# Three kinds of 128-row tiles moved from three 256-column products per weight block to one of 512 and one of 256

## What is computed

```
u = rmsnorm(x) @ w_in                       # layer 1; z is a slice of 4096 columns of u
y = concat(y_l, y_m) * silu(z);  x = x + y @ w_out
u = rmsnorm(x) @ w_in                       # layer 2
z, xbc, dt = split(u);  y = ssd(xbc, dt) * silu(z);  x = x + norm(y) @ w_out
u = rmsnorm(x) @ w_in                       # layer 3; last 3 * 2048 columns: branch gates g0, g1, g2
mix = sigmoid(g0) * s5(u) + sigmoid(g1) * gla(u) + sigmoid(g2) * diff(u)
```

## Time and profile before

| | |
|---|---|
| median of 3 runs | 3216.04 us (3215.46 to 3218.31) |
| the profiled execution: its time, its span | 3217.17 us, 3215.4 us |
| granted TensorE clock, mean | 0.988 |
| busy, share of the span | TensorE 96%, its weight loads 89%, VectorE 72%, ScalarE 57%, GpSimd 17% |
| HBM, mean over the span | 173 GB/s |

### The profile page before, as it was taken

The page is one execution under the profiler, slowest core; times in us unless marked ns, Lnnn a source line. Parts: engine busy times, 40 slices in busy tenths (PEclk is TensorE's granted clock), DMA queues, the critical chain, the costliest instruction groups (busy, mean ns, idle before and its releaser), DMA issues.

```text
span 3215.4 us, 53602 instructions
## 1 busy us (share of the span) xinstructions
PE 3089.6 (96%) x21726; PEld 2853.5 (89%) x21726; DVE 2301.2 (72%) x3156; ACT 1830.6 (57%) x2363; POOL 532.8 (17%) x640
## 2 busy tenths in 40 slices
PE   7999898999999999999988999999999999999998
PEld 6889888889999999889877899999998888888886
DVE  6655788657778877675866787786656888888544
ACT  5554677645666676645556454444445666666443
POOL 2000000000000000114743565760001000000000
PEclk9999999999999999999999999999999999999999
DMA  5445434556555555556433444456555555555554
GB/s 198 141 155 179 142 133 142 198 191 217 181 174 184 178 177 201 192 177 208 156 115 112 142 153 157 170 173 210 184 184 190 190 190 190 190 190 190 190 190 138
DMA packets 158473, 560.50 MB, mean 174 GB/s; under 512 B 17600, under 2 KB 25856, under 8 KB 157712
## 3 DMA queue, kind: packets, MB, share of 16 engines
q1 hardware_dynamic: 158224, 557.06, 51.8%
HBM read 550.64 MB, written 6.36 MB: 173 GB/s over the span
## 4 chain that ended last, share of the span: by engine, by line
PE 67%; DVE 17%; ACT 10%; issue 3%; POOL 2%; DMA 0%; SPq 0%; DVEq 0%; ACTq 0%; POOLq 0%
PE ps L565 67%; DVE WL L1336 5%; ACT WH L912 3%; ACT L902 3%; DVE XV L1310 2%; DVE YB L1310 1%; ACT DB L902 1%; DVE XV L1306 1%; DVE YS L1299 1%; DVE DB L1299 1%; ACT RS L902 1%; DVE XP L1299 0%; POOL PB L1922 0%; DVE ZB L1299 0%; DVE XC L1310 0%
## 5 line engine op out<-in xcount | busy, mean ns | idle before, releaser
L565 PE MATMUL ps<-XN,WH 128*128 128x256 f32 (+1 forms) x8864 | 1855.8, 303 | 34.2 <-DVE XN L1310 17.7
L912 ACT ACTIVATE WH<-RAW 128x1024 fp32r<-128x1024 f32 x1010 | 1064.9, 1058 | 1119.7 <-PE ps L565 1078.9
L1336 DVE TENSOR_TENSOR WL<-RAW,WH 128x1024 fp32r<-128x1024 f32 x1010 | 1259.6, 1253 | 444.8 <-ACT WH L912 439.3
L565 PEld LDWEIGHTS ps<-XN,WH 128*128 128x128 f32 x8864 | 1434.2, 192 | 112.9 <-DVE XN L1310 18.6
L565 PE MATMUL ps<-XN,WL 128*128 128x256 f32 x5120 | 1444.5, 282 | 0.0
L565 PEld LDWEIGHTS ps<-XN,WL 128*128 128x128 f32 x5120 | 980.9, 192 | 0.0
L565 PE MATMUL ps<-YS,WH 128*128 128x512 f32 (+1 forms) x1088 | 372.9, 390 | 9.7 <-DVE WL L1336 5.1
L565 PE MATMUL ps<-YS,WL 128*128 128x256 f32 x1056 | 297.3, 281 | 0.0
L1922 POOL TENSOR_TENSOR RSB<-RSB,SQ 128x256 f32<-128x256 f32 x75 | 75.9, 1012 | 1224.7 <-ACT SQ L902 1223.5
L565 PEld LDWEIGHTS ps<-YS,WH 128*128 128x128 f32 x1088 | 204.5, 190 | 55.3 <-DVE WL L1336 6.7
L565 PE MATMUL ps<-HS,WH 128*128 128x512 f32 x688 | 238.6, 392 | 0.0
(11 more groups left out here) (332 smaller groups left out, 3347.2 us busy)
## 6 DMA issues: line engine op xcount, KB each, us to landing
RAW<-in_w SPq DMA_DIRECT2D x1010, 512.0 KB, 3.4
CSB<-sums SPq DMA_DIRECT2D x64, 128.0 KB, 3.8
X<-scratch SPq DMA_DIRECT2D x2, 2048.0 KB, 8.2
X<-in_x SPq DMA_DIRECT2D x4, 512.0 KB, 8.3
X<-in_x SPq DMA_DIRECT2D x1, 2048.0 KB, 8.0
scratch<-X SPq DMA_DIRECT2D x1, 2048.0 KB, 8.6
scratch<-X SPq DMA_DIRECT2D x4, 512.0 KB, 5.4
out<-X SPq DMA_DIRECT2D x4, 512.0 KB, 2.6
```

What stands on the lines that cost most here:

```text
L565: return pe.e.matmul(dst, l, r, start=start, stop=stop, skip_group_check=True)
L912: act.e.activation(WH[:, w % NH, :], RAW[:, w % NB, :], ACT.Copy).then_inc(*act.one(("wh", w)))
L1336: dve.e.tensor_tensor(WL[:, w % NB, :], RAW[:, w % NB, :], WH[:, w % NH, :].bitcast(F32), SUB).then_inc(*dve.one(("wl", w)))
```

## The change

The z, zs and g0 tiles get form "w". Their evacuation becomes four instructions on three engines, spread over more steps: at s = 0 ScalarE copies the second half out of PSUM (`second_half`, into ZLO, ZSLO or G0LO); at s = 1 VectorE adds the first half to it (`halves`, which also frees the bank) and GpSimd multiplies by RSB, in place of VectorE's `evac` at s = 0; at s = 2 ScalarE takes Silu or Sigmoid; VectorE's product with Silu(z) goes from s = 1 to s = 3. `gg`'s product on VectorE goes from its first step to s = 2, and `gl`'s steps come one later. Each copy waits until the add before it has read the one buffer.

```diff
@@ STEPS @@
-    "xm": 2, "q": 3, "k": 3, "v": 3, "o": 1, "gates": 7, "z": 2, "lruc": 3, "xl": 2, "zl": 1, "ra": 1, "ix": 1,
-    "tail": 6, "heads": 64, "eo": 1, "dt": 1, "dts": 9, "xv": 1, "zs": 1, "ssd": 21, "oo": 1, "nx": 4,
+    "xm": 2, "q": 3, "k": 3, "v": 3, "o": 1, "gates": 7, "z": 4, "lruc": 3, "xl": 2, "zl": 1, "ra": 1, "ix": 1,
+    "tail": 6, "heads": 64, "eo": 1, "dt": 1, "dts": 9, "xv": 1, "zs": 3, "ssd": 21, "oo": 1, "nx": 4,
...
-    "dv": 1, "dq": 1, "diff": 15, "g12": 1, "gb": 1, "db": 1, "g0": 1, "gg": 1, "gl": 2, "s5": 207, "wo": 1,
+    "dv": 1, "dq": 1, "diff": 15, "g12": 1, "gb": 1, "db": 1, "g0": 3, "gg": 3, "gl": 3, "s5": 207, "wo": 1,
@@ plan @@
-        p.append(whole(tile("z", (j,), "e_w_in", 6144 + 128 * j), 16))
+        p.append(whole(tile("z", (j,), "e_w_in", 6144 + 128 * j, form="w"), 16))
-            p.append(whole(tile("zs", (g, j), "o_w_in", 512 * g + 128 * j), 16))
+            p.append(whole(tile("zs", (g, j), "o_w_in", 512 * g + 128 * j, form="w"), 16))
-        p.append(whole(tile("g0", (n,), "w_in_2", 7184 + 128 * n), 16))
+        p.append(whole(tile("g0", (n,), "w_in_2", 7184 + 128 * n, form="w"), 16))
@@ scalar @@
+            def second_half(dst, *id_):
+                act.wait_ge(*at("tile", *id_))
+                fn(dst, bank(*id_)[:, 256:512], ACT.Copy, ("half",) + id_)
             def z(j, s):
-                if s == 0 and j % 4 == 3:
+                if s == 0:
+                    if j:
+                        act.wait_ge(*at("za", j - 1))
+                    second_half(ZLO, "z", j)
+                if s == 2 and j % 4 == 3:
                     act.wait_ge(*at("zq", j))
                     fn(ZQ, ZQ, ACT.Silu, ("zs", j // 4))
             def zs(g, j, s):
-                if j == 3:
+                if s == 0:
+                    if g + j:
+                        act.wait_ge(*at("zsa", *((g, j - 1) if j else (g - 1, 3))))
+                    second_half(ZSLO, "zs", g, j)
+                if s == 2 and j == 3:
                     act.wait_ge(*at("zsr", g))
                     fn(ZB, ZB, ACT.Silu, ("zsd_", g))
             def g0(n, s):
-                act.wait_ge(*at("g0r", n))
...
+                if s == 0:
+                    act.wait_ge(*(at("g0a", n - 1) if n else at("sy", 31)))
+                    second_half(G0LO, "g0", n)
+                if s == 2:
+                    act.wait_ge(*at("g0r", n))
...
@@ vector @@
+            def halves(dst, *id_, name):
+                dve.wait_ge(*at("half", *id_))
+                tt(dst, bank(*id_)[:, 0:256], dst_half(id_[0]), ADD, ("free",) + id_, name)
             def z(j, s):
-                if s == 0:
-                    evac(ZQ[:, j % 4, :], 0, "z", j, more=[("zq", j)])
-                if s == 1 and j % 4 == 3:
+                if s == 1:
+                    halves(ZQ[:, j % 4, :], "z", j, name=("za", j))
+                if s == 3 and j % 4 == 3:
...
             def zs(g, j, s):
-                evac(ZB[:, j, :], 1, "zs", g, j, more=[("zsr", g)])
+                if s == 1:
+                    halves(ZB[:, j, :], "zs", g, j, name=("zsa", g, j))
             def g0(n, s):
-                evac(SG[:, 2 * (n % 2), :], 2, "g0", n, more=[("g0r", n)])
+                if s == 1:
+                    halves(SG[:, 2 * (n % 2), :], "g0", n, name=("g0a", n))
             def gg(n, s):
+                if s != 2:
+                    return
...
             def gl(n, s):
-                if s == 0:
+                if s == 1:
...
-                if s == 1:
+                if s == 2:
@@ gpsimd @@
+            def z(j, s):
+                if s == 1:
+                    pool.wait_ge(*at("za", j))
+                    pool.wait_ge(*at("rs", 0))
+                    tt(ZQ[:, j % 4, :], ZQ[:, j % 4, :], RSB, MUL, ("zq", j))
+            def zs(g, j, s):
+                if s == 1:
+                    pool.wait_ge(*at("zsa", g, j))
+                    pool.wait_ge(*at("rs", 1))
+                    tt(ZB[:, j, :], ZB[:, j, :], RSB, MUL, ("zsr", g))
+            def g0(n, s):
+                if s == 1:
+                    pool.wait_ge(*at("g0a", n))
+                    pool.wait_ge(*at("rs", 2))
+                    tt(SG[:, 2 * (n % 2), :], SG[:, 2 * (n % 2), :], RSB, MUL, ("g0r", n))
```

More of the change, by code:

```diff
@@ L391, in build @@
         ONER = m("ONER", 256, rows=4)
+        ZLO = m("ZLO", 256)
         top_at = (end - 2304) // 32 * 32
@@ L431, in build @@
         CSB = [m(f"CSB{i}", 256) for i in range(NCSB)]
+        ZSLO = m("ZSLO", 256)
         assert m.at <= XT + 2048
@@ L485, in build @@
         MAG = P1[2]
+        G0LO = flat(CR)[:, 0:256]
         OB = v3(m("OB", 512), 2)
@@ L1238, in g0 @@
             def g0(n, s):
-                act.wait_ge(*at("g0r", n))
-                sl = SG[:, 2 * (n % 2), :]
-                fn(sl, sl, ACT.Sigmoid, ("g0s", n))
+                if s == 0:
[3 more added lines that the diff above has]
+                    act.wait_ge(*at("g0r", n))
+                    sl = SG[:, 2 * (n % 2), :]
+                    fn(sl, sl, ACT.Sigmoid, ("g0s", n))
             def gg(n, s):
+                if s:
+                    return
                 act.wait_ge(*at("tile", "gg", n))
@@ L1434, in gates, with dst_half @@
                     copy(AT, bank("gt")[:, 0:8], ("rc",), ("free", "gt"))
+            def halves(dst, *id_, name):
+                dve.wait_ge(*at("half", *id_))
+                tt(dst, bank(*id_)[:, 0:256], dst_half(id_[0]), ADD, ("free",) + id_, name)
+            def dst_half(kind):
+                return {"z": ZLO, "zs": ZSLO, "g0": G0LO}[kind]
             def z(j, s):
-                if s == 0:
-                    evac(ZQ[:, j % 4, :], 0, "z", j, more=[("zq", j)])
-                if s == 1 and j % 4 == 3:
+                if s == 1:
+                    halves(ZQ[:, j % 4, :], "z", j, name=("za", j))
+                if s == 3 and j % 4 == 3:
                     dve.wait_ge(*at("zs", j // 4))
@@ L1572, in zs @@
             def zs(g, j, s):
-                if g == 0 and j == 0:
-                    dve.wait_ge(*at("cst"))
-                evac(ZB[:, j, :], 1, "zs", g, j, more=[("zsr", g)])
+                if s == 1:
+                    if g == 0 and j == 0:
+                        dve.wait_ge(*at("cst"))
+                    halves(ZB[:, j, :], "zs", g, j, name=("zsa", g, j))
             def ssd(g, s):
@@ L2000, in gpsimd @@
                 "wo": lambda n, s: squares(3, n), "dn": lambda n, s: squares(4, n), "heads": heads, "ssd": ssd,
-                "s5": s5})
+                "s5": s5, "z": z, "zs": zs, "g0": g0})
         def sync(e):
```

## The result

The changed kernel is **slower**: 3237.85 us in the median of 6 runs (3233.68 to 3242.0), against 3218.05 us for the kernel before (6 runs, 3215.46 to 3220.23). The ratio is 1.0063, with a 95% interval of 1.0052 to 1.0074: about 20 us, where I had forecast a gain of 9. The profiled execution spans 3237.5 us, 22.1 more than that of before.

What follows compares the result with a forecast made beforehand. TensorE was taken as the limit, VectorE close behind in layer 2. 13.7 - 0.8 - 0.2 - 1.5 - 0.7 - 1.6 = 8.9 us gained, so 3208.3 profiled and 3207.1 us forecast, range 3202 to 3213.5.

Steps and rivals of the forecast that it cites:

- TensorE's gain: In z, zs and g0: 13.4 ns saved per block by one matmul fewer, 13.7 us in all.
- the Trainium skill's rule: Matmuls saved in z, zs, g0: 2.5 ns each, 2.6 us; near the rival "A matmul less is worth nothing", chance 0.03.
- The wait for RC: In z: TensorE's wait on RC grows from 1.4 to 2.2 us, a loss of 0.8.
- The SBUF port: Layer 2: GpSimd's products slow VectorE by 0.05 us each, two ahead of the second mask in seven groups, loss 0.7 us.
- the slower rival: Mainly layer 2: GpSimd's product takes the port ahead of VectorE, costing 24 us, so 3230 us; chance 0.06.
- my bound: Layer 2: at most, one GpSimd product holds VectorE for its whole length, 1.0 us.
- Layer 2, the wait for DB: Mask 0.53 us earlier, TensorE 0.75 earlier; seven waits grow by 0.22 to 1.8 us, loss 1.5.
- The clock: In z, layer 2 and g0: granted clock 1.00 throughout, so no term for it.
- g0(5)'s bank: In g0: VectorE frees this bank late for g0(6), a loss of 1.6 us, once.
- The masks of heads seven and eight: Layer 2, late releases rival: these masks delay TensorE, eating most of the gain, 3211 to 3212.5 us; chance 0.20.
- WL in layer 2: Sign on VectorE: WL at 1.22 to 1.25 us as forecast; 1.5 us and more would show the port.
- A new wait in another place, or a clock below 1.00 where it was 1.00: Sign, anywhere in the kernel: either would make the whole sum wrong.

Runs made afterwards that it cites:

- the later step: TensorE issues the first two heads' products of each layer 2 group one unit later; changed kernel so edited 3207.18 us, kernel before so edited 3204.12 us.
- without the product: The changed kernel with GpSimd's products by the rows' factors left out for z, zs and g0; 3223.23 us.
- GpSimd's product added: The kernel before plus one GpSimd product of 256 columns, never read, behind each zs product of VectorE; 3228.8 us.
- add ahead of WL: The changed kernel, but in layer 2 VectorE adds the halves ahead of that unit's WL, not behind it; 3233.29 us.
- product on VectorE: The changed kernel with the product by the rows' factors on VectorE right behind the add, in place of GpSimd; 3234.65 us.
- nx spread: The kernel with g0 alone by 512 columns, with the four steps of nx on every second unit; 3221.95 us.

## Why the prediction was wrong

**TensorE's gain: real, but smaller.** The 346.6 ns of the up tiles don't hold in layer 2. From the zs tiles of the changed kernel with the later step, where TensorE hardly waits:

```profile
1047.73 0.40 PE L568 MATMUL ps<-XN,WH 128*128 128x512 f32 x1
...
1048.08 0.40 PE L568 MATMUL ps<-XN,WH 128*128 128x512 f32 x1
...
1048.42 0.40 PE L568 MATMUL ps<-XN,WH 128*128 128x512 f32 x1
...
1048.79 0.40 PE L568 MATMUL ps<-XN,WH 128*128 128x512 f32 x1
```

Most blocks start 349 to 350 ns apart, about a quarter of them 361. At the full clock the mean over the zs tiles is 351 to 352 in every kernel that has the form there, against 359.7 in xv and zs tiles before. In z it is 347.7 in the changed kernel and 352.9 with z alone (360 before), in g0 350.1 (359.6 before). For the changed kernel that makes 3.1 + 4.1 + 2.4 = about 9.7 us where I had counted 13.7. The groups agree: in the pair with the later step YS starts every 63.46 us without the form and every 63.01 with it; with the one wait of 0.4 us, 0.07 per group, taken off, that is 0.5 us less, against the 0.86 counted. Why some blocks are 361 ns apart wasn't settled. Per matmul saved that is 7 to 12 ns: less than my 13.4, and more than the 2.5 of the Trainium skill's rule (TensorE: Matmul & The Clock Gate, "Back-to-back issue gap"), whose 2.6 us isn't borne out either.

**z: waits right, total not.** The wait for RC became 2.0 (2.2 expected), but a half-clock stretch stood on it, 1.7 us for which I had no term. (In the kernel with z alone it stands there too; in two later kernels with the same wait of 2.0 us it doesn't.)

**The failed step: "The SBUF port".** I took "the measured mean" of 0.05 us per product, 0.7 us in all. It was 0.56 us per product, twice ahead of each second mask: 7.8 us in the seven waits. The mean of rows 10 comes from products that fall beside VectorE's instructions anyhow; here a product and VectorE's next instruction are released by the same add every time. I wrote just this down in favour of the slower rival ("GpSimd starts at the very moment VectorE takes up its next instruction") and gave it 6%. That rival had the right mechanism: its threshold for a gain, 0.4 us per product, was passed. But its sum doesn't give the measured time. It counts 24 products (the third, ahead of the eighth head, never made TensorE wait), and with 24 times 0.56 it comes to about 3220; the rest up to 3238 is the clock, the waits at wo and behind the groups, and TensorE's smaller gain. The Trainium skill (SBUF — State Buffer, "Who interferes with whom") says that the two exclude each other for an instruction's length, and that the issue order decides who blocks. The traces agree on both: 1.11 us masks beside a 0.72 us product, and a product of 1.64 us behind a WL. Only the size of my bound was off: the product takes 0.73 us when it comes first; the row that I took, 1012 ns, is a mean over products of 0.7 to 1.75 us.

**"Layer 2, the wait for DB": too small.** The mask's end moved by the 0.53 us counted, TensorE's arrival by 1.07 and not 0.75, so arrival added 0.54 us per wait and not 0.22. Its 0.32 more isn't explained by the blocks, which gained less than counted; where it comes from stays open.

**The clock: no term, and the largest one.** "The granted clock is 1.00 in all these stretches, so no term comes from it" holds for the kernel before. Outside these stretches that kernel has 79 us at half the clock, all at or just behind waits of TensorE, most of them 2 us and longer; those rows I didn't use. In layer 2, with seven waits in each profile:

| waits for DB | kernel | half-clock stretches |
|---|---|---|
| 1.6 us | before, z alone, g0 alone | 0, 0, 0 |
| 2.0 to 2.2 | without the product | 1 |
| 2.5 (one 3.0) | GpSimd's product added | 4 |
| 2.7 to 2.9 | add ahead of WL | 4 |
| 3.1 to 3.4 | changed, zs alone | 5, 5 |
| 3.0 to 3.5 | product on VectorE | 6 (at five waits) |

So a wait that grows from 1.6 to 3.3 us cost 1.7 and, in five of seven, 1.7 again. The port's 7.8 us brought most of the clock's 8.5 us in layer 2 with it: the kernel without the product has four stretches fewer there, 6.8 us. The table isn't a rule of length alone: with nx spread one wait of 2.4 us drew a stretch, and elsewhere in the kernel before two waits of 1.7 and 1.8 us did:

```profile
24.96:28.37 3.41, 3.41 (x18) 0.50 0.09 13
1799.89:1803.30 3.41, 3.41 (x13) 0.50 0.02 5
```

**g0: the first wait right, the second not seen.** For g0(5)'s bank I said 1.6 us, it was 2.1. At wo I had none: gl's product moved from step 0 to step 1, so it frees the last gl's bank a unit later, and wo's tiles want that bank at once. I had checked the release in z, zs and behind nx, not at the end of the stage. 2.6 us more wait, and 6.8 us at half the clock. Every kernel here that keeps g0 as before has 0.9 us there.

**The rivals.** The masks of heads seven and eight never made TensorE wait, and WL in layer 2 stayed at 1.22 us, as said. "A new wait in another place, or a clock below 1.00 where it was 1.00" was named as what would break the sum; both came.

## What to carry to other kernels

An engine shared through a port isn't priced by a mean over chance meetings when the edit makes the two start together; look at what its releaser releases on the other engine. Before TensorE's work is made shorter in a stretch where it already waits for a chain, move the wait: here two numbers in TensorE's list of steps gave 14 us, and only then can the shorter work pay. And price a wait of TensorE that an edit lengthens at its growth and up to 1.7 us more for the clock, as the table shows it: none of 21 waits of 1.6 to 1.7 us in layer 2 drew a stretch, one of seven at 2.0 to 2.2, five of seven at 3.1 to 3.4.

## What the runs showed of the hardware

Two things that I hadn't expected. GpSimd's product of 256 columns has two durations, 0.73 us where it starts with VectorE's instruction and 1.64 where a WL is ahead of it, and in the second case it still holds the instruction behind that WL for 0.34 us. And the half-clock stretches: in the profiles of before and of the change each is 3.41 or 6.83 us long, but for the last one at the end of the span, and lies at or just behind a wait of TensorE, though not at every wait of the same length (five of seven at 3.1 to 3.4 us, one of seven at 2.0 to 2.2). Their number differs from one kernel's profile to the next even where no edit reaches: in the first 225 us it is between one and three of 3.41 us over the fourteen profiles. So one stretch more or less, 1.7 us, in a single profile says nothing.
